# A three-part transformer block on one core: the opening rewritten, the sigmoid table loaded earlier, evictions moved ahead of weight splits

## The chip, the cores and the metric

The kernel runs on one NeuronCore of a Trainium2 chip. The metric is the device time of one execution in microseconds (us). TensorE does the matmuls, VectorE (DVE in the profile), ScalarE (ACT) and GpSimd (POOL) the rest, and SyncE (SP) issues most of the DMAs.

## The reference

Input x is 256 tokens by 1024 features, all fp32. The part that matters here is the first block's start, a recurrent branch, and beside it keys and values from a memory `mem_2` of 256 tokens:

```python
h = h + recurrent_block(rmsnorm(h, a_norm), a_w_in, a_conv_w, a_conv_b, a_w_gate, a_b_gate, a_lambda, a_w_out)

def recurrent_block(x, w_in, conv_w, conv_b, w_gate, b_gate, lam, w_out):
    u = x @ w_in
    gate, rec = u[..., :D_RNN], u[..., D_RNN:]
    rec = causal_depthwise_conv(rec, conv_w, conv_b)
    h = rg_lru(rec, w_gate, b_gate, lam)      # two sigmoids of rec @ w_gate, exp, sqrt, a scan over the tokens
    return (jax.nn.gelu(gate) * h) @ w_out
```

Behind it come an MLP of width 4096, a block of banded attention with another such MLP, and a third block with three kinds of attention, three gated branches, and a gated convolutional FFN of width 2816. None of that is touched by the change.

## The kernel before

**Numbers.** Every product is done in three passes. A weight w is split into a high part (a copy in the type fp32r, made by ScalarE) and a low part (w minus the high part, made by VectorE). The activations are split in the same way into the two halves of the tiles XA and XB. The product is then high times high, low times high and high times low.

**Weights.** They come in 163 units of 1 MB (128 x 2048), one after another, through four slots of `raw`, `whi` and `wlo`. SP issues the load of unit u once VectorE has finished the low part of unit u-4 (semaphore `s_lo`). ScalarE's `split(u)` (L617 to L638) waits for the landing, and for TensorE to be done with the slot; VectorE's `split(u)` (L1669 to L1690) waits for ScalarE's. Every engine's program is written out by hand in a fixed order. A split is done LEAD = 3 units ahead: while TensorE works on unit u, the splits of unit u+3 stand between the evictions of u. In the order of units, 0 to 3 are the recurrent half of `a_w_in` (U_REC), 4 the first quarter of its gate half, 5 the LRU gate weights (U_LRU), 6 to 8 the rest of the gate half, 9 and 10 the memory's keys (U_MEMK, called MEMK below), 11 and 12 its values (U_MEMV), 13 to 16 `a_w_out`.

**The opening.** SP loads x (L458), then unit 0 in two halves (L467), then seven of the small vectors (`BY_SP`), then units 1 to 3, then the memory rows (L488). ScalarE issues eleven small loads (L708), does four squares with a sum (L662) of x for the first norm, splits unit 0 in two halves (L716), copies the transposed vectors out of PSUM (L718) and makes the high parts of XA (L725). POOL makes the reciprocal roots (`roots`, L514 to L520), VectorE scales x (`norm`, L1698). TensorE runs matmuls of the identity with itself (`keep_warm`, L1195) until the data is there, transposes the two token halves of x (L1205), and between them, after waiting for all 18 small loads, the vectors (L1208 to L1211). VectorE makes the low parts of unit 0 (L1760) and of XA (L1765), then all of unit 1 (L1690). TensorE runs unit 0 with the contraction as its outer loop (L1222), then a small matmul for a table of biases (L1229), then units 1 to 4.

**The gates.** The products of U_REC are evicted by ScalarE (`rec_unit`, L736), convolved by VectorE (`conv`, L1789) and split into XB by `conv_hi` (ScalarE, L747) and `conv_lo` (VectorE, L1803). Then come eight gate products n = 0 to 7 (L1235 to L1246); product n waits for its low part (`s_cl`), and from n = 4 on for the two sigmoids of n-4 (L1239), because they share PSUM banks. The sigmoids are L784. `gate_out` (L752) evicts the groups of units 4 and 6 to 8, groups 8 to 15. The groups of MEMK, 16 to 19, need groups 12 to 15 out of their banks (L1083). `squares(SQ_NORM[1])` squares the memory rows on ScalarE (L662), `norm_hi` (L695) makes the high parts of XB for them, `decay` (L757) is exp and tanh, and L797 is the square root that `scan` (L1834) on VectorE waits for.

The lines before in ScalarE's order around the gates:

```python
split(U_GATE[0] + LEAD)
conv_hi(3)
act.wait_ge(s_ew, 32)
gate_out(0)
for n in range(8):
    ...
split(U_LRU + LEAD)
```

Of the kernel before, what the change touches and what calls it, by code (L numbers as in the profile page):

```python
# [13 lines left out]
P = 128  # L14
# [85 lines left out]
ROOTS = [2 * i for i in range(9)]  # L100
SUMS = [4 * i for i in range(7)] + [None, 28]
# [36 lines left out]
def bass_blocks(nc, A, out):  # L138
# [57 lines left out]
    with ctx:  # L196
# [112 lines left out]
        s_hi0, s_lo0, s_gain = sem("first_unit_half_hi"), sem("first_unit_half_lo"), sem("norm_gains")  # L309
        s_mem = sem("mem_loaded")  # L310
# [59 lines left out]
        BY_SP, BY_ACT = 7, 11  # L370
        WARM_UP, WARM_KEEP = 18, 4
# [53 lines left out]
        small_loads = []  # L425

        def small(dst, src):
            small_loads.append(lambda queue: queue.dma_start(dst, src).then_inc(s_small, 16))

        def vec(name, row, n):  # L430
            src = A[name].rearrange("a n -> (a n)") if len(A[name].shape) == 2 else A[name]
            small(rows_in[row:row + n, 0, :], src.rearrange("(k n) -> k n", n=P))

        vec("a_norm", R_ANORM, 8)
        vec("kv_norm", R_KV, 8)
        vec("b_norm", R_B, 8)
        vec("mlp_norm", R_MLP, 16)
        vec("norm_mix_pre_2", R_MIX, 8)
        vec("norm_ffn_pre_2", R_FFN, 8)
        vec("norm_mem_2", R_MEM, 8)  # L440
        vec("a_conv_b", R_CB, 8)
        small(rows_in[R_CW:R_CW + 32, 0, :], A["a_conv_w"][0].rearrange("w (k n) -> (w k) n", n=P))
        vec("a_lambda", R_LAM, 8)
        small(rows_in[R_BG:R_BG + 16, 0, :], A["a_b_gate"][0].rearrange("b (k n) -> (b k) n", n=P))
        fw = A["ffn_conv_w_2"][0].rearrange("w (k n) -> (w k) n", n=P)
        small(rows_in[0:88, 1, :], fw[0:88])
        small(rows_in[0:44, 2, :], fw[88:132])
        small(rows_in[44:88, 2, :], A["ffn_conv_b_2"][0].rearrange("(k n) -> k n", n=P))
        for r, name in enumerate(("k_norm", "b_q_norm")):
            src = A[name] if r == 0 else A[name][0]  # L450
            for half_ in range(2):
                small(rows_in[r:r + 1, 3, 64 * half_:64 * half_ + 64], src.rearrange("(a n) -> a n", a=1))
# [3 lines left out]
        def _(sp):  # L456
# [41 lines left out]
        def _(pool):  # L498
# [23 lines left out]
            def roots_deferred(b, col, power):  # L522

                pool.wait_ge(s_ss, 4 * b + 4)
# [11 lines left out]
            roots(SQ_NORM[0])  # L536
# [72 lines left out]
        def _(act):  # L609
# [43 lines left out]
            def squares(b, src, ready):  # L653

                for i, (t, c, bank) in enumerate(pieces()):
# [64 lines left out]
            act.wait_ge(s_xnT, XT_OF[0] + 1)  # L720
            for k in range(KT):
# [45 lines left out]
            rec_unit(1)  # L767
            conv_hi(0)
# [1496 lines left out]
```

## Time and profile before

| what | value |
|---|---|
| runs before | 1027.12, 1028.32, 1030.39 us; median 1028.32 |
| the profiled execution's own time | 1027.62 us |
| its span, from the first to the last instruction | 1025.7 us |
| TensorE's mean granted clock | 0.995 of full speed |
| busy share of TensorE, VectorE, ScalarE, POOL | 97%, 68%, 53%, 8% |
| share of the chain that ended last | PE 87%, DVE 7%, ACT 3%, issue 2%, DMA 1% |

"Busy" of TensorE counts a matmul from its start to a modelled end, so matmuls that follow each other without a gap show as 100%. In the timeline, "x2" merges neighbouring instructions of a kind; the bracket at the end of a row is the idle time just before it and what ended that by the profile. L-numbers are lines of the kernel.

### The profile page before, as it was taken

To read this page: it belongs to the slowest core of one execution; us is meant where nothing else is said; L and a number is where in the kernel's file an instruction comes from. 1 tells how busy PE (TensorE), PEld (TensorE's weight loads), DVE (VectorE), ACT (ScalarE), POOL (GpSimd) and SP (SyncE) were. 2 spreads that over 40 slices of the span, in tenths; PEclk is the share of its full clock that TensorE was granted. 3 is DMA by queue.
4 is the path that set the end of the run, shared out by engine and by line. 5 is a ranking of instruction groups with operands and counts; after the bars stand their busy time and mean duration, and the time that the engine had idled before them with its cause. 6 is when DMAs were issued, how large, how long until landed. Compare 5 with 4: busy or idle time off the path is not lost.

```text
span 1025.7 us, 15612 instructions
## 1 busy us (share of the span) xinstructions
PE 999.3 (97%) x6234; PEld 885.6 (86%) x6234; DVE 699.6 (68%) x1023; ACT 548.6 (53%) x804; POOL 83.8 (8%) x104
## 2 busy tenths in 40 slices
PE   8999999999999989999999999999999989999997
PEld 7998888888887866888888899989999879999996
DVE  5969566565667588575656565488665759877775
ACT  6897454444446477454444453356554456545452
POOL 2710010000002210020000000000004210000000
PEclk9999999999999999999999999999999999999999
DMA  9736586555535614565555647453454625655531
GB/s 319 227 122 206 166 316 214 172 196 200 170 122 176 235 50 165 183 219 173 196 201 169 203 124 234 135 165 125 124 165 152 226 75 188 223 174 197 179 110 41
DMA packets 120306, 180.39 MB, mean 176 GB/s; under 512 B 3145, under 2 KB 93609, under 8 KB 120249
## 3 DMA queue, kind: packets, MB, share of 16 engines
q1 hardware_dynamic: 118384, 174.11, 51.2%
q0 software_dynamic: 1536, 5.36, 1.5%
q8 instruction: 40, 0.66, 0.3%
q10 hardware_dynamic: 329, 0.12, 0.1%
q14 instruction: 17, 0.14, 0.0%
HBM read 178.48 MB, written 1.10 MB: 175 GB/s over the span
## 4 chain that ended last, share of the span: by engine, by line
PE 87%; DVE 7%; ACT 3%; issue 2%; DMA 1%; SPq 0%; POOL 0%; DVEq 0%; POOLq 0%; ACTq 0%
PE PS L1090 29%; PE PS L1154 28%; PE PS L1097 11%; PE PS L1099 5%; DVE wlo L1690 3%; PE PS L1347 2%; PE PS L1304 2%; PE PS L1444 2%; PE PS L1143 1%; PE PS L1594 1%; DVE arena L1795 1%; PE PS L1426 1%; PE PS L1395 1%; PE PS L1124 1%; DMA arena<-in_norm_mem 1%
## 5 line engine op out<-in xcount | busy, mean ns | idle before, releaser
L1690 DVE TENSOR_TENSOR wlo<-raw,whi 128x2048 fp32r<-128x2048 f32 x154 | 354.3, 2305 | 122.7 <-ACT whi L638 122.1
L638 ACT ACTIVATE whi<-raw 128x2048 fp32r<-128x2048 f32 x153 | 291.9, 1910 | 140.2 <-PE PS L1154 100.4
L1090 PE MATMUL PS<-XA,whi 128*128 128x256 f32 x1520 | 278.0, 285 | 0.3 <-DVE wlo L1690 0.3
L1090 PEld LDWEIGHTS PS<-XA,whi 128*128 128x128 f32 x1520 | 237.6, 192 | 3.9 <-issue 1.7
L1090 PE MATMUL PS<-XA,wlo 128*128 128x256 f32 x760 | 214.9, 283 | 0.0
L1154 PE MATMUL PS<-whi,XB 128*128 128x512 f32 x736 | 209.4, 391 | 0.7 <-DVE XB L1887 0.7
L1097 PE MATMUL PS<-XA,whi 128*128 128x512 f32 x512 | 182.1, 398 | 0.0
L1154 PEld LDWEIGHTS PS<-whi,XB 128*128 128x128 f32 x736 | 135.3, 188 | 29.3 <-issue 1.0
L1090 PEld LDWEIGHTS PS<-XA,wlo 128*128 128x128 f32 x760 | 145.6, 192 | 0.0
L1099 PE MATMUL PS<-XA,wlo 128*128 128x256 f32 x512 | 143.7, 281 | 0.0
L1154 PE MATMUL PS<-wlo,XB 128*128 128x512 f32 x368 | 117.6, 390 | 0.0
L1097 PEld LDWEIGHTS PS<-XA,whi 128*128 128x128 f32 x512 | 96.2, 188 | 23.6 <-issue 0.4
L1099 PEld LDWEIGHTS PS<-XA,wlo 128*128 128x128 f32 x512 | 96.7, 189 | 1.1
L1154 PEld LDWEIGHTS PS<-wlo,XB 128*128 128x128 f32 x368 | 69.1, 188 | 14.6
L827 ACT ACTIVATE arena<-PS 128x256 f32<-128x256 f32 x64 | 24.2, 381 | 89.1 <-PE PS L1099 89.0
L1876 DVE TENSOR_TENSOR arena<-PS,arena 128x256 f32<-128x256 f32 x64 | 26.4, 420 | 38.4 <-ACT arena L827 38.4
L1090 PE MATMUL PS<-XB,whi 128*128 128x256 f32 x256 | 46.4, 284 | 1.6 <-issue 1.6
L1304 PE MATMUL PS<-whi,XA 128*128 128x512 f32 x128 | 43.9, 408 | 1.0 <-DVE wlo L1690 1.0
L1055 ACT ACTIVATE arena<-arena,fvec 128x256 f32<-128x256 f32 x44 | 25.6, 596 | 35.2 <-DVE arena L2214 35.2
L1090 PEld LDWEIGHTS PS<-XB,whi 128*128 128x128 f32 x256 | 39.9, 192 | 2.0 <-issue 2.0
L2200 DVE SCALAR_TENSOR_TENSOR arena<-arena,fvec 128x256 f32<-128x256 f32 x88 | 38.6, 481 | 1.4 <-ACT arena L1055 0.7
L526 POOL TENSOR_SCALAR ss<-ss 128x1 f32<-128x1 f32 x8 | 2.5, 308 | 438.3 <-ACT arena L692 437.9
(240 smaller groups left out, 1223.3 us busy)
## 6 DMA issues: line engine op xcount, KB each, us to landing
raw<-in_w_up SPq DMA_DIRECT2D x32, 1024.0 KB, 5.5
raw<-in_w_down SPq DMA_DIRECT2D x32, 1024.0 KB, 4.9
raw<-in_w_ffn_up SPq DMA_DIRECT2D x22, 1024.0 KB, 5.0
raw<-in_w_in SPq DMA_DIRECT2D x21, 1024.0 KB, 5.1
raw<-in_w_ffn_down SPq DMA_DIRECT2D x11, 1024.0 KB, 4.8
raw<-in_w_kv SPq DMA_DIRECT2D x8, 1024.0 KB, 5.0
raw<-in_a_w_in SPq DMA_DIRECT2D x7, 1024.0 KB, 7.8
raw<-in_w_mem_kv SPq DMA_DIRECT2D x4, 1024.0 KB, 5.0
```

What stands on the lines that cost most here:

```text
L638: act.activation(whi[:, s, :], raw[:, s, :], ACT.Copy).then_inc(s_hi, 1)
L827: act.activation(dst, PS[:, bank_of(g), T:2 * T], ACT.Copy).then_inc(s_low, 1)
L1055: act.activation(fc[:, f, :], fu[:, f, 2:2 + T], ACT.Identity, scale=fvec[:, 1, c:c + 1], bias=fvec[:, 1, 44 + c:45 + c]).then_inc(s_fc, 1)
L1090: ins = pe.matmul(PS[:, bank_of(g), 0:T], w[:, k, P * m:P * m + P], X[:, k0 + k, part, :], start=(i == 0 and part == 0 and w is hi), stop= ...
L1097: pe.matmul(PS[:, bank, :].rearrange("p (e n) -> p e n", e=2), hi, x, start=opens, stop=False, skip_group_check=True)
L1099: return pe.matmul(PS[:, bank, 0:T], lo, x[:, 0, :], start=False, stop=closes, skip_group_check=True)
L1154: return pe.matmul(PS[:, bank + n * t + c, 0:width], X[:, k0 + k, part, P * t:P * t + P], w[:, k, c0 + 512 * c:c0 + 512 * c + width], star ...
L1304: ins = pe.matmul(PS[:, t_banks[t], :], X[:, 4 * i + k, part_, P * t:P * t + P], w[:, k, :], start=(i == 0 and k == 0 and part_ == 0 and w ...
L1347: ins = pe.matmul(PS[:, Q_BANKS[t][c], :], XB[:, 2 * i + k, part_, P * t:P * t + P], w[:, k, 512 * c:512 * c + 512], start=(i == 0 and k = ...
L1690: dve.tensor_tensor(wlo[:, s, :], raw[:, s, :], whi[:, s, :].bitcast(F32), ALU.subtract).then_inc(s_lo, 1)
L1876: dve.tensor_tensor(dst, PS[:, bank_of(g), 0:T], dst, ALU.add).then_inc(s_evac, 1)
L2200: ins = dve.scalar_tensor_tensor(fc[:, f, :], fu[:, f, i:i + T], fvec[:, 0, c:c + 1], fc[:, f, :], ALU.mult, ALU.add)
```

## The change

The first norm's squares go half to ScalarE (columns 0 to 511) and half to VectorE (512 to 1023, a multiply with a running sum), with semaphores of their own, and POOL waits for both. `a_norm` is loaded first, by ScalarE, and transposed and copied on its own ahead of x's transposes; the other vectors are transposed between unit 0 and unit 1 and copied after split(2). A dummy square ahead of ScalarE's other small loads brings the first table in; SP has ten small loads, ScalarE seven besides a_norm. The load of the memory rows goes from behind unit 3 to behind unit 5. Units 0 and 1 are both split in halves, the halves woven into XA's high parts, and TensorE runs both with the contraction outermost. The matmuls of `keep_warm` are 15, 3 and 3 instead of 18 and 4. A dummy sigmoid after `rec_unit(1)` brings the sigmoid table in. `conv_hi(3)` goes from ahead of the sigmoids to behind those of n = 1, `gate_out(0)` behind them all; `gate_out(2)` and `gate_out(3)` go ahead of the splits they stood behind. On VectorE `conv_lo(3)` goes ahead of `split(U_GATE[0] + LEAD)`.

```diff
-        BY_SP, BY_ACT = 7, 11
-        WARM_UP, WARM_KEEP = 18, 4
+        N_SMALL = 17
+        WARM_UP, WARM_BETWEEN, WARM_KEEP = 15, 3, 3
@@ SP
                 if u == 0:
-                    for load_small in small_loads[:BY_SP]:
-                        load_small(sp)
-                if u == 3:
+                    for dst, src in SMALL_BY_SP:
+                        sp.dma_start(dst, src).then_inc(s_small, 16)
+                if u == 5:

                     sp.wait_ge(s_xnT, 1)
@@ POOL
-            roots(SQ_NORM[0])
+            for t in range(TT):
+                pool.wait_ge(s_sq0, t + 1)
+                pool.wait_ge(s_sq1, t + 1)
+                link(pool.tensor_scalar(ss[:, 4 + t:5 + t], ss[:, 2 * t:2 * t + 1], ss[:, 2 * t + 1:2 * t + 2], EPS, ALU.add,
+                                        ALU.add))
+                pool.tensor_tensor(rstd[:, t:t + 1], ss[:, 4 + t:5 + t], mhalf[:, 0:1], ALU.pow).then_inc(s_root0, 1)
@@ ScalarE
-            for load_small in small_loads[BY_SP:]:
-                load_small(act)
-
-
-            squares(SQ_NORM[0], res, lambda i: act.wait_ge(s_x[i // 2], 16))
-            for h, done in enumerate((s_hi0, s_hi)):
-                act.wait_ge(s_landed[0] if h else s_w0, 16)
+            dst, src = vec("a_norm", R_ANORM, 8)
+            act.dma_start(dst, src).then_inc(s_an, 16)
+            act.wait_ge(s_zero, 1)
+            act.activation(snmax[:, 0, 0:1], smax[:, 0, 0:1], ACT.Square)
+            for dst, src in SMALL_BY_ACT:
+                act.dma_start(dst, src).then_inc(s_small, 16)
+
+            def first_half(w, h, done):
+
                 at = slice(UNIT // 2 * h, UNIT // 2 * h + UNIT // 2)
-                act.activation(whi[:, 0, at], raw[:, 0, at], ACT.Copy).then_inc(done, 1)
-            act.wait_ge(s_vT, 1)
-            act.activation(vecs[:], PS[:, 6, 0:P], ACT.Copy).then_inc(s_gain, 1)
+                act.activation(whi[:, w, at], raw[:, w, at], ACT.Copy).then_inc(done, 1)
+
+            for t in range(TT):
+                act.wait_ge(s_x[t], 16)
+                act.activation(av[:, 4 * t:4 * t + 2, :].rearrange("p a b -> p (a b)"), res[:, t, 0:512], ACT.Square,
+                               scale=D ** -0.5, accum_out=ss[:, 2 * t:2 * t + 1]).then_inc(s_sq0, 1)
+            act.wait_ge(s_w0, 16)
+            first_half(0, 0, s_hi0)
+            act.wait_ge(s_anT, 1)
+            act.activation(vecs[:, R_ANORM:R_ANORM + 8], PS[:, 6, 448:456], ACT.Copy).then_inc(s_gain, 1)
...
-                if k == 4:
-                    split(1, part=0)
-            split(1, part=1)
+                if k == 3:
+                    act.wait_ge(s_landed[0], 16)
+                    first_half(0, 1, s_hi)
+                if k == 5:
+                    act.wait_ge(s_landed[1], 16)
+                    first_half(1, 0, s_hi0)
+            first_half(1, 1, s_hi)
             split(2)
+            act.wait_ge(s_vT, 1)
+            act.activation(vecs[:, 8:P], PS[:, 6, 8:P], ACT.Copy).then_inc(s_vecs, 1)
+            act.wait_ge(s_vecs, 1)
...
             rec_unit(1)
+            act.activation(snmax[:, 0, 0:1], smax[:, 0, 0:1], ACT.Sigmoid)
             conv_hi(0)
...
             split(U_GATE[0] + LEAD)
-            conv_hi(3)
-
             act.wait_ge(s_ew, 32)
-            gate_out(0)
             for n in range(8):

+                if n == 2:
+                    conv_hi(3)
...
                 ins.then_inc(s_lru, 1)
+            gate_out(0)
...
+            gate_out(2)
             split(U_GATE[2] + LEAD)
-            gate_out(2)
...
+            gate_out(3)
             split(U_GATE[3] + LEAD)
-            gate_out(3)
@@ TensorE
             keep_warm(WARM_UP)
+            pe.wait_ge(s_an, 16)
+            pe.transpose(PS[:, 6, 448:456], rows_in[0:8, 0, :], ident[0:8, 0:8]).then_inc(s_anT, 1)
             for t in range(TT):
...
                 if t == 0:
-                    pe.wait_ge(s_small, 16 * (BY_SP + BY_ACT))
+                    keep_warm(WARM_BETWEEN)
+            ins.then_inc(s_xnT, 1)
+            keep_warm(WARM_KEEP)
+            for u in range(2):
...
+                if u == 0:
+
+                    pe.wait_ge(s_small, 16 * N_SMALL)
+                    pe.wait_ge(s_gain, 1)
                     pe.transpose(PS[:, 6, 0:P], rows_in[:, 0, :], ident[:])
...
+                    pe.wait_ge(s_tables, 16 * 4)
+                    pe.matmul(PS[0:16, 7, 0:384], relb[0:32, :], onehot[0:32, :], start=True, stop=True).then_inc(s_eps, 1)
+
+            for i in range(2, 4):
                 unit_a(U_REC[i], G_REC[i])
@@ VectorE
+            dve.memset(smax[:, 0, 0:1], 0.0).then_inc(s_zero, 1)
...
+                dve.tensor_tensor_reduce(junk, v, v, 1.0 / D, 0.0, ALU.mult, ALU.add, ss[:, 2 * t + 1:2 * t + 2])\
+                   .then_inc(s_sq1, 1)
...
-            split(1)
+            first_lo(1, 0, s_hi0, s_lo0)
+            first_lo(1, 1, s_hi, s_lo)
+            dve.wait_ge(s_vecs, 1)
             dve.tensor_copy(fvec[:, :, :], PS[:, 6, P:P + 176].rearrange("p (a b) -> p a b", a=2))
...
+            conv_lo(3)
             split(U_GATE[0] + LEAD)
-            conv_lo(3)
```

## Rows read from the trace of the kernel before

**Rows 1.** The page, part 1: busy time and share of the span, by engine.

```profile
PE 999.3 (97%) x6234; PEld 885.6 (86%) x6234; DVE 699.6 (68%) x1023; ACT 548.6 (53%) x804; POOL 83.8 (8%) x104
```

**Rows 2.** Timeline of TensorE: start and length in us, engine, line, operation.

```profile
11.59 1.97 PE L1205 MATMUL PS<-ident,arena 128*128 128x128 f32 x8
...
21.94 0.51 PE L1090 MATMUL PS<-XA,whi 128*128 128x256 f32 x2 [0.26 <-DVE wlo L1690]
...
45.08 0.28 PE L1243 MATMUL PS<-XB,whi 128*128 128x256 f32 x1
...
50.12 0.35 PE L1243 MATMUL PS<-XB,whi 128*128 128x256 f32 x1 [2.01 <-DVE XB L1806]
...
73.90 0.48 PE L1090 MATMUL PS<-XB,whi 128*128 128x256 f32 x2 [1.61 <-issue]
```

**Rows 3.** Busy time in two stretches: length, engines, granted clock, DMA share, GB/s.

```profile
12.20:12.80 0.60, 0.60 (x5) 0.60 (x4) 0.25 (x1) 0.00 (x0) 0.60 (x2) 0.50 1.11 362
26.00:35.00 9.00, 9.00 (x78) 9.00 (x77) 8.86 (x14) 7.43 (x13) 8.09 (x11) 1.00 0.89 281
```

**Rows 4.** The chain that ended last, two of its pieces before 120 us.

```profile
5.08 5.87 DMA arena<-in_norm_mem
...
85.64 31.48 PE PS L1154 x138
```

**Rows 5.** Timeline of ScalarE from 44 us on.

```profile
44.14 1.90 ACT L638 ACTIVATE whi<-raw 128x2048 fp32r<-128x2048 f32 x1
46.47 0.81 ACT L750 ACTIVATE XB<-arena 128x256 fp32r<-128x256 f32 x2 [0.42 <-DVE arena L1795]
47.19 0.64 ACT L643 ACTIVATE arena<-PS 128x256 f32<-128x256 f32 x2
47.85 1.28 ACT L784 ACT_TABLE_LOAD   x1
49.14 5.94 ACT L784 ACTIVATE arena<-PS,vecs 128x256 f32<-128x256 f32 x16
...
71.62 1.90 ACT L638 ACTIVATE whi<-raw 128x2048 fp32r<-128x2048 f32 x1
...
130.48 0.62 ACT L692 ACTIVATE arena<-res 128x512 f32<-128x512 f32 x1
```

**Rows 6.** Timeline of ScalarE in the opening.

```profile
5.15 1.28 ACT L662 ACT_TABLE_LOAD   x1 [5.15 <-issue]
6.44 0.63 ACT L662 ACTIVATE arena<-res 128x512 f32<-128x512 f32 x1
...
8.91 1.99 ACT L716 ACTIVATE whi<-raw 128x1024 fp32r<-128x1024 f32 x2
...
13.66 0.84 ACT L725 ACTIVATE XA<-PS,vecs 128x256 fp32r<-128x256 f32 x2 [1.69 <-PE PS L1205]
```

**Rows 7.** Timeline of POOL and of VectorE in the opening.

```profile
9.96 0.57 POOL L520 TENSOR_TENSOR rstd<-ss,mhalf 128x1 f32<-128x1 f32 x1
10.56 0.75 DVE L1698 TENSOR_SCALAR arena<-res,rstd 128x1024 f32<-128x1024 f32 x1 [0.85 <-POOL rstd L520]
...
21.80 0.33 DVE L1768 COPY fvec<-PS 128x176 f32<-128x176 f32 x1
```

**Rows 8.** DMA issues of small windows: size of one, us from issue to landing.

```profile
res<-in_x SPq DMA_DIRECT2D x1, 512.0 KB, 3.7
...
res<-in_x SPq DMA_DIRECT2D x1, 512.0 KB, 4.7
...
raw<-in_a_w_in SPq DMA_DIRECT2D x1, 1024.0 KB, 13.1
...
arena<-in_mem SPq DMA_DIRECT2D x1, 1024.0 KB, 8.7
```

**Rows 9.** Groups by line and shape: VectorE's multiply-reduce, busy us, mean ns.

```profile
L1972 DVE CUSTOM_DVE_ANT_0 arena<-PS,arena 128x256 f32<-128x256 f32 x32 | 13.4, 420 | 0.0
```

**Rows 10.** Timeline of VectorE from 76 us on.

```profile
76.48 1.23 DVE L1838 TENSOR_TENSOR arena<-arena 128x1024 f32<-128x1024 f32 x1 [0.63 <-ACT arena L797]
...
88.42 2.28 DVE L1690 TENSOR_TENSOR wlo<-raw,whi 128x2048 fp32r<-128x2048 f32 x1
```

More of the change, by code:

```diff
@@ L99 @@
 SQ_POST = [6, 8]
-ROOTS = [2 * i for i in range(9)]
-SUMS = [4 * i for i in range(7)] + [None, 28]
+ROOTS = [None] + [2 * i for i in range(8)]
+SUMS = [None] + [4 * i for i in range(6)] + [None, 24]
 KO = [0, 4, 1, 5, 2, 6, 3, 7]
@@ L423, in bass_blocks, with row_of @@
         NORM_HI = [8 * n + (8 if n > 3 else 0) for n in range(8)]
-        small_loads = []
-        def small(dst, src):
-            small_loads.append(lambda queue: queue.dma_start(dst, src).then_inc(s_small, 16))
+        def row_of(A_):
+            return A_.rearrange("a n -> (a n)") if len(A_.shape) == 2 else A_
         def vec(name, row, n):
-            src = A[name].rearrange("a n -> (a n)") if len(A[name].shape) == 2 else A[name]
-            small(rows_in[row:row + n, 0, :], src.rearrange("(k n) -> k n", n=P))
@@ L434, in bass_blocks @@
[L434 to L444, printed above, removed]
@@ L445, in bass_blocks @@
-        fw = A["ffn_conv_w_2"][0].rearrange("w (k n) -> (w k) n", n=P)
[L446 to L452, printed above, removed]
+            return rows_in[row:row + n, 0, :], row_of(A[name]).rearrange("(k n) -> k n", n=P)
@@ L455, in _ @@
+        SMALL_BY_SP = (vec("kv_norm", R_KV, 8), vec("b_norm", R_B, 8), vec("mlp_norm", R_MLP, 16),
+                       vec("norm_mix_pre_2", R_MIX, 8), vec("norm_ffn_pre_2", R_FFN, 8), vec("norm_mem_2", R_MEM, 8))
+        for r, src in enumerate((A["k_norm"], A["b_q_norm"][0])):
+            SMALL_BY_SP += tuple((rows_in[r:r + 1, 3, 64 * e:64 * e + 64], src.rearrange("(a n) -> a n", a=1)) for e in range(2))
         @block.sync
@@ L522, in roots_deferred @@
             def roots_deferred(b, col, power):
-                pool.wait_ge(s_ss, 4 * b + 4)
+                pool.wait_ge(s_ss, SUMS[b] + 4)
                 for t in range(TT):
@@ L1206, in _ @@
                 if t == 0:
-                    pe.wait_ge(s_small, 16 * (BY_SP + BY_ACT))
+                    keep_warm(WARM_BETWEEN)
+            ins.then_inc(s_xnT, 1)
+            keep_warm(WARM_KEEP)
+            for u in range(2):
+                g = G_REC[u]
+                hi, lo = W8(whi, u % SLOTS), W8(wlo, u % SLOTS)
+                for k in range(KT):
+                    if k % 4 == 0:
+                        pe.wait_ge(*((s_lo0, u + 1) if k == 0 else (s_lo, u + 1)))
+                    if u == 0:
+                        pe.wait_ge(s_xlo, NORM_HI[0] + k + 1)
+                    for m in range(2):
+                        for w, part in ((hi, 0), (hi, 1), (lo, 0)):
+                            ins = pe.matmul(PS[:, bank_of(g + m), 0:T], w[:, k, P * m:P * m + P], XA[:, k, part, :],
+                                            start=(k == 0 and part == 0 and w is hi), stop=(k == KT - 1 and w is lo),
+                                            skip_group_check=True)
+                        if k == KT - 1:
+                            ins.then_inc(s_step, 1)
+                if u == 0:
+                    pe.wait_ge(s_small, 16 * N_SMALL)
+                    pe.wait_ge(s_gain, 1)
                     pe.transpose(PS[:, 6, 0:P], rows_in[:, 0, :], ident[:])
@@ L1211, in _ @@
                     pe.transpose(PS[:, 6, 384:386], rows_in[0:2, 3, :], ident[0:2, 0:2]).then_inc(s_vT, 1)
-            ins.then_inc(s_xnT, 1)
-            keep_warm(WARM_KEEP)
-            u, g = U_REC[0], G_REC[0]
-            hi, lo = W8(whi, u % SLOTS), W8(wlo, u % SLOTS)
-            for k in range(KT):
-                if k % 4 == 0:
-                    pe.wait_ge(*((s_lo0, 1) if k == 0 else (s_lo, u + 1)))
-                pe.wait_ge(s_xlo, NORM_HI[0] + k + 1)
-                for m in range(2):
-                    for w, part in ((hi, 0), (hi, 1), (lo, 0)):
-                        ins = pe.matmul(PS[:, bank_of(g + m), 0:T], w[:, k, P * m:P * m + P], XA[:, k, part, :],
-                                        start=(k == 0 and part == 0 and w is hi), stop=(k == KT - 1 and w is lo),
-                                        skip_group_check=True)
-                    if k == KT - 1:
-                        ins.then_inc(s_step, 1)
-            pe.wait_ge(s_tables, 16 * 4)
-            pe.matmul(PS[0:16, 7, 0:384], relb[0:32, :], onehot[0:32, :], start=True, stop=True).then_inc(s_eps, 1)
-            for i in range(1, 4):
+                    pe.wait_ge(s_tables, 16 * 4)
+                    pe.matmul(PS[0:16, 7, 0:384], relb[0:32, :], onehot[0:32, :], start=True, stop=True).then_inc(s_eps, 1)
+            for i in range(2, 4):
                 unit_a(U_REC[i], G_REC[i])
```

29 lines of the change are left out of this document (24 added, 5 removed).

## The prediction

> **What bounds the kernel now.** I read the page first: TensorE is busy for 97% of the span [rows 1]. So nothing counts unless it moves TensorE's work forward in time, and after the opening a microsecond gained or lost stays to the end. Next TensorE's own timeline, for its gaps [rows 2]: between the first matmul and 75 us it waits three times: 0.26 at 21.94 ahead of unit 1 (for the weight's low part), 2.0 at 50.12 after the fourth of the eight gate products, which began at 45.08, and 1.6 at 73.90 ahead of the first MEMK product. Then the windows [rows 3]: from 26 to 35 us VectorE is busy 8.86 of 9.00 us. VectorE sets the pace there, not ScalarE (7.43). Its order is split, convolution, low parts, four times over, all without a gap; whatever it gains at the opening arrives whole at the gate products. The chain [rows 4] adds that the opening starts with a wait for the last small load, landing at 10.95, and that from 85.64 TensorE runs 138 wide matmuls in a row, 0.228 us each.
>
> The wait at 50.12 needs care. The trace names VectorE's L1806, but the product that waits is n=4, and that needs the sigmoids of n=0 (L1239). They begin at 49.14, because of an eviction of 0.64 and a table load of 1.28 ahead of them [rows 5]; a pair takes 5.94/8 = 0.74, so they end at 49.9. Both causes end together; to gain here, both must go, and the change moves both. The wait at 73.90 is for the eviction of group 12, which stands at 73.42 behind a split that starts at 71.62 [rows 5].
>
> **The opening, part by part.** Before [rows 6]: table load 5.15, four squares from 6.44 at 0.63 each, the last accumulator read near 9.0; POOL's second root ends at 10.53, VectorE's second xn runs 10.56 to 11.31 [rows 7], and the second transposes end at 13.56, with a granted clock of 0.50 (1.2 GHz) [rows 2, 3]. ScalarE's first XA high part is at 13.66 [rows 6].
>
> After: ScalarE issues one load (0.6), then does the table load and a dummy square (1.5), then seven loads (before they and four others filled 0.73 to 5.12, about 0.40 each, so 2.9). If these are serial, its first square starts at 5.8; if the loads are issued while the table loads, at 4.5, when x lands (0.73 + 3.7) [rows 8]. The second half of x lands 5.9 (1.17 + 4.7). VectorE does the other two squares: 128x512 isn't in the trace; L1972 takes 0.42 for 256 elements [rows 9], so between 0.42 and 0.84 plus its read of 0.08. I take 0.7, hidden beside ScalarE in the serial case. ("Lead" below is how much earlier than before the same work comes.) Serial: both ScalarE squares end at 7.2; POOL's two roots, 0.95 and 1.42 as before, end at 9.1; xn of the second half ends at 9.9, 1.4 earlier. Without the four small transposes (0.5) in between, the second transposes start at 10.0. They take 1.1 at the full clock and 1.97 at the lower level. So the first XA high part is at 11.15 or 12.0, a lead of 2.5 or 1.65.
>
> From there to fvec (21.80 before, 8.14 after the first high part [rows 6, 7]) the same work runs, in other order: unit 0's second half (1.0, from 1.99 for two [rows 6]) now stands between ScalarE's high parts 3 and 4, and VectorE waits 0.55 for it; unit 1 in halves recovers the 0.47 that VectorE waited for its whole split; and VectorE waits 0.4 more for the vector copy, now behind split(2). Net 0.6 lost. **VectorE's lead after the opening: 1.9 (full clock) or 1.05 (lower), serial.** With the loads under the table load, the roots start 1.3 earlier but the second half of x lands only at 5.9, so xn is 0.9 earlier: 2.75 or 1.9. I take 1.9, the value that two of the four combinations give.
>
> TensorE: unit 0 starts at 12.3 but waits for VectorE's parts, ends near 18.7; four transposes (0.66) and L1229 (0.8) now stand between unit 0 and 1, so unit 1 starts at 20.2 instead of 21.94, lead 1.75. Unit 1 with its high and low halves is fed in time.
>
> The moved DMAs: SP issues ten small loads instead of seven ahead of unit 1, 1.2 us later at most, one of them (a_norm) gone to ScalarE. Unit 3 was issued from 6.25 and landed 13.1 later [rows 8], units 1 to 3 landing 3 us apart at 13.3, 16.3, 19.3: the stream is full, so the delay costs between 0 and 1.2, covered by 1.5 us until ScalarE takes each. The mem load moves behind units 4 and 5 and their waits; it took 8.7 to land [rows 8], would land near 29, and its first reader comes at 39.8. Units 4 and 5 land 3 us earlier. Nothing.
>
> **The gate products.** Leads 1.9 (VectorE) and 1.75 (TensorE): the products start at 43.35, n=3 ends at 46.2. ScalarE's split(7), at 44.14 before [rows 5], now ends at 44.1; sigmoids 0 and 1 follow at 44.2 (the sigmoid table is loaded after rec_unit(1), where ScalarE waited 1.26 for VectorE). Then conv_hi(3), whose source VectorE finished at 46.8 - 1.9 = 44.9, then sigmoids 2 to 7. n=4 finds the sigmoids of n=0 at 45.0; conv_lo(3) without unit 7's split (2.2) ahead of it ends at 46.9, and n=6 wants it at 47.6. So the 2.0 wait is gone, the eight end at 49.1 against 53.1, and TensorE's lead is 4.0.
>
> ScalarE: 44.2 + 5.7 (sigmoids) + 0.72 (conv_hi) + 0.64 (gate_out(0)) = 51.3 at the next split, which stood at 54.85: **ScalarE's lead 3.6** (1.9, plus the table load 1.28, plus 0.43 that it waited at 46.47). gate_out(0) is free where it is now: group 12 needs it at 56. Everything on ScalarE up to 71.62 moves with it. There gate_out(2) comes first: group 12 is out at 68.0 + 0.5 = 68.5, TensorE arrives at 72.3 - 4.0 = 68.3. MEMK starts 5.4 earlier. gate_out(3), due for TensorE at 74.2, is out at 74.1.
>
> **What is late next.** VectorE's chain from the square root: 76.48 multiply, then scans, unit 11, y, and unit 12's split ending at 90.7, with no gap [rows 10]. It hangs on ScalarE's square root, which keeps its place behind norm_hi, one split and one eviction: lead 3.6. TensorE wants unit 12 24 x 0.228 = 5.5 after 85.54, at 91.05: slack 0.35. With a lead of 5.4 it arrives at 85.6 and unit 12 is ready at 87.1. It waits 1.5, and keeps 3.6 + 0.35 = **4.0 us**, to the end: behind it TensorE is the bound and the others wait for it.
>
> **Sum.** 1027.62 (profiled run; span 1025.70 and 1.92 around it) - 4.0 = 1023.6. The median of the runs shown is 0.7 above that run, so I give 1028.3 - 4.0 = **1024.3**. The four combinations of the opening give 3.1, 4.0, 4.0 and 4.9.
>
> On the table: between ScalarE's instruction before it and its first sigmoid lie 1.28 us and no more (47.85 to 49.14 [rows 5]). The Trainium skill, "ScalarE: Activation LUTs", What ACT_TABLE_LOAD costs, puts a drain of 1.38 on top of 1.28; by that the hoisted load would be worth 2.66 and the sum 1.4 more. The trace doesn't show that drain.
>
> **Rivals.**
> *The opening's lead is lost.* TensorE now waits for a_norm ahead of all transposes. It is issued first, but if it lands as late as the last small load did (10.95 [rows 4]), the first high part comes at 14, VectorE's lead is -0.8 and the gain 1.3: 1027.0. Against it: it stands ahead of every other load on its queue. Chance 0.12.
> *Square reloads a table.* Squares of the mem rows now run after the sigmoid table is in. If that set lacks Square, two loads of 1.28 come back: gain 4.0 - 2.55 = 1.45, 1026.9. Against it: Squares run at 130.48 without a load, long after a Gelu table came in [rows 5]. Chance 0.06. The Trainium skill's same page, Table sets, names copy, identity, relu and abs as present in every set and tells to batch by set; Square isn't among those it names.
> *TensorE keeps all.* If unit 12 is ready anyway, because VectorE's tail has slack that I read as work, the gain is 5.3: 1023.0. Against it: that stretch shows no idle time. Chance 0.05.
> *Slower.* The start-up has 21 filler matmul calls instead of 22 and other gaps. The clock fell to 0.50 at 11.6 and was back at 15.2, under the first matmuls. If it stays at the lower level through unit 0, that unit's 48 matmuls take 5.76 more (0.12 to 0.24): unit 1 starts at 26.0, the gain is used up (n=4 at 52.05 against 50.12, less the wait of 1.6): nothing gained. If it stays through unit 1 too, another 5.76: 1034. This decides only from 5.8 us of delay on. Against it: matmuls without a gap brought it back in 3 us before. Chance 0.05.
> *The forecast.* 0.72, its own range 1023.4 to 1025.2.
>
> **How the numbers follow.** A measurement of this kernel can tell about 0.3% (3.1 us) from no change: faster is below 1025.2. Of the forecast's 0.72, 0.60 lie there (its slow-clock serial end and run-to-run spread fall short). Faster 0.60 + 0.05 = 0.65; same 0.12 + 0.12 + 0.06 = 0.30; slower 0.05. The range goes from 1023.0 less the runs' spread of 0.7, 1022.3, to the first rival's 1027.0.
>
> **What would show it.** First square near 4.5 or 5.8; first XA high part at 11 to 12; fvec copy at 19 to 20.8; no table load between split(7) and the first sigmoid, and no wait over 0.3 in the gate products; MEMK's first matmul at 68.5; a new TensorE wait of 1 to 2 us near 85.6 ahead of unit 12, released by L1690's counterpart. If that wait is missing the gain is over 5; if a table load stands ahead of the mem squares, or a_norm lands after 8, it is under 2. Behind 95 us the two traces should run parallel; a gain that shrinks there makes the forecast wrong.

## The result and the profile after

The changed kernel takes **1023.31 us** in the median of 5 runs (1022.90 to 1024.28), against 1028.34 for the kernel before in 5 runs (1027.12 to 1030.39): a ratio of 0.995, 95% interval 0.9937 to 0.9963. The profiled execution took 1023.31 with a span of 1021.1; the profiled one of before took 1027.62 with 1025.7. So the two profiles differ by 4.6 in the span, the medians by 5.0; when both were run again (below), the medians differed by 4.2. 1024.3 was predicted, with a range of 1022.3 to 1027.0.

On the page the busy times have hardly moved [rows 1]; the span lost idle time of TensorE:

```profile
PE 998.4 (98%) x6233; PEld 884.8 (87%) x6233; DVE 704.3 (69%) x1029; ACT 547.9 (54%) x803; POOL 85.1 (8%) x104
```

TensorE's timeline (start, length, engine, line, operation, idle time before it) answers to [rows 2]. There are the two groups of transposes, the first product of unit 0, the first of unit 1, the first gate product, the first MEMK product, the first MEMV product (unit 11) and the first of unit 13:

```profile
7.70 1.09 PE L1222 MATMUL PS<-ident,arena 128*128 128x128 f32 x8
...
9.30 1.09 PE L1222 MATMUL PS<-ident,arena 128*128 128x128 f32 x8
...
11.72 0.47 PE L1237 MATMUL PS<-XA,whi 128*128 128x256 f32 x2 [0.65 <-DVE XA L1807]
...
19.42 0.50 PE L1237 MATMUL PS<-XA,whi 128*128 128x256 f32 x2
...
42.55 0.28 PE L1266 MATMUL PS<-XB,whi 128*128 128x256 f32 x1
...
67.67 0.47 PE L1105 MATMUL PS<-XB,whi 128*128 128x256 f32 x2 [0.19 <-issue]
...
81.11 0.47 PE L1169 MATMUL PS<-whi,XB 128*128 128x512 f32 x1 [1.71 <-ACT kT_me L641]
...
92.10 0.61 PE L1169 MATMUL PS<-whi,XA 128*128 128x512 f32 x2
```

The waits of 2.0 and 1.6 are gone. A new one of 1.71 stands ahead of MEMV, not of unit 12. The second group of transposes takes 1.09, not 1.97: the granted clock is 1.00 from 9.30 to 10.39, where it was 0.50 for the same work [rows 3].

ScalarE's timeline answers to [rows 5, 6]. The small loads (rows of ACTq) are issued while the table loads; the sigmoid table comes in at 26.70, and the squares of the memory rows at 38.97 and the sigmoids at 43.53 have no table load ahead of them:

```profile
1.38 1.28 ACT L709 ACT_TABLE_LOAD   x1 [1.38 <-PEq L2298]
1.45 0.28 ACTq L711 DMA_DIRECT2D arena<-in_a_conv_b  x1
...
4.94 0.63 ACT L720 ACTIVATE arena<-res 128x512 f32<-128x512 f32 x1 [2.07 <-DMA res<-in_x]
...
10.50 0.84 ACT L732 ACTIVATE XA<-PS,vecs 128x256 fp32r<-128x256 f32 x2 [1.45 <-PE PS L1222]
...
26.70 1.28 ACT L782 ACT_TABLE_LOAD   x1
27.99 0.20 ACT L782 ACTIVATE snmax<-smax 128x1 f32<-128x1 f32 x1
...
38.97 0.62 ACT L660 ACTIVATE arena<-arena 128x512 f32<-128x512 f32 x1
...
41.42 1.90 ACT L636 ACTIVATE whi<-raw 128x2048 fp32r<-128x2048 f32 x1
43.53 1.58 ACT L798 ACTIVATE arena<-PS,vecs 128x256 f32<-128x256 f32 x4 [0.20 <-PE PS L1268]
...
50.40 2.05 ACT L636 ACTIVATE whi<-raw 128x2048 fp32r<-128x2048 f32 x1
...
76.62 2.01 ACT L818 ACTIVATE arena<-arena 128x1024 f32<-128x1024 f32 x2
78.53 1.90 ACT L636 ACTIVATE whi<-raw 128x2048 fp32r<-128x2048 f32 x1
80.33 0.64 ACT L641 ACTIVATE kT_me<-PS 128x256 f32<-128x256 f32 x2
```

VectorE's timeline answers to [rows 7, 10]: the first of its two squares, the fvec copy, the multiply behind the square root, and unit 12's split. The last two come 4.43 earlier than before.

```profile
4.50 0.69 DVE L1786 CUSTOM_DVE_ANT_0 arena<-res 128x512 f32<-128x512 f32 x1 [3.58 <-DMA res<-in_x]
...
19.08 0.34 DVE L1812 COPY fvec<-PS 128x176 f32<-128x176 f32 x1 [0.32 <-ACT vecs L743]
...
72.05 1.23 DVE L1882 TENSOR_TENSOR arena<-arena 128x1024 f32<-128x1024 f32 x1
...
83.99 2.28 DVE L1713 TENSOR_TENSOR wlo<-raw,whi 128x2048 fp32r<-128x2048 f32 x1
```

**Where the time came from.** VectorE's lead at fvec is 21.80 - 19.08 = 2.72. ScalarE's next split after the sigmoids stood at 54.85 and now stands at 50.40: lead 4.45, that is 2.72 plus 1.73 gained at the gates. The table load gives 1.29 of that and conv_hi(3)'s wait 0.42; 0.22 comes from instructions standing closer together, and 0.2 is lost in the new wait at 43.53. TensorE's lead at unit 13 is 96.54 - 92.10 = 4.44. The spans differ by 4.6, so nothing is given back behind it.

**The edge.** Four rows of the kernel before show why TensorE keeps 4.44. First its ScalarE, then its TensorE, at the point of the new wait:

```profile
73.42 0.65 ACT L643 ACTIVATE arena<-PS 128x256 f32<-128x256 f32 x2
...
84.76 0.64 ACT L643 ACTIVATE kT_me<-PS 128x256 f32<-128x256 f32 x2
```

```profile
85.54 0.47 PE L1154 MATMUL PS<-whi,XB 128*128 128x512 f32 x1
96.54 0.62 PE L1154 MATMUL PS<-whi,XA 128*128 128x512 f32 x2
```

The first MEMV product waits for MEMK's keys to be evicted into kT_me. It started 0.78 behind that eviction's start (85.54 - 84.76); in the changed kernel also 0.78 (81.11 - 80.33). Before, TensorE came at the same instant, so the timeline showed no idle time. Both go back to one eviction, that of group 12 at 73.42: TensorE starts MEMK 0.48 behind it and MEMV 11.64 after that, and ScalarE reaches kT_me 11.34 after it; 0.48 + 11.64 - 11.34 is 0.78. So the eviction of kT_me stood on the edge all along, and TensorE can be no earlier than it.

### The profile page after: what moved, and what is told of

Its sections match the earlier page's. It is cut to its first block, busy times and chain, and to the rows that moved or that the text cites. A ratio compares the mean times of both kernels' runs of the same rounds, so it can differ in the third digit from the quotient of the medians.

```text
span 1021.1 us, 15617 instructions
## 1 busy us (share of the span) xinstructions
PE 998.4 (98%) x6233; PEld 884.8 (87%) x6233; DVE 704.3 (69%) x1029; ACT 547.9 (54%) x803; POOL 85.1 (8%) x104
## 3 DMA queue, kind: packets, MB, share of 16 engines
q0 software_dynamic: 1536, 5.36, 1.6%
## 4 chain that ended last, share of the span: by engine, by line
PE 88%; ACT 6%; DVE 4%; issue 2%; POOL 0%; DVEq 0%; POOLq 0%; ACTq 0%
PE PS L1169 28%; PE PS L1105 28%; PE PS L1112 11%; PE PS L1114 5%; PE PS L1370 2%; PE PS L1327 2%; PE PS L1467 2%; PE PS L1158 1%; DVE wlo L1713 1%; PE PS L1617 1%; PE PS L1449 1%; ACT whi L636 1%; PE PS L1237 1%; PE PS L1418 1%; PE PS L1139 1%
## 5 line engine op out<-in xcount | busy, mean ns | idle before, releaser
L1105 PE MATMUL PS<-XA,whi 128*128 128x256 f32 x1488 | 272.2, 285 | 0.0
L1105 PEld LDWEIGHTS PS<-XA,whi 128*128 128x128 f32 x1488 | 232.6, 192 | 3.0 <-issue 1.7
L1105 PE MATMUL PS<-XA,wlo 128*128 128x256 f32 x744 | 210.4, 283 | 0.0
L1114 PE MATMUL PS<-XA,wlo 128*128 128x256 f32 x512 | 143.7, 281 | 0.0
L1105 PEld LDWEIGHTS PS<-XA,wlo 128*128 128x128 f32 x744 | 142.5, 192 | 0.0
L1112 PEld LDWEIGHTS PS<-XA,whi 128*128 128x128 f32 x512 | 96.2, 188 | 23.8 <-issue 0.4
L1114 PEld LDWEIGHTS PS<-XA,wlo 128*128 128x128 f32 x512 | 96.7, 189 | 1.1
```

The lines of the kernel that those rows point to most:

```text
L1105: ins = pe.matmul(PS[:, bank_of(g), 0:T], w[:, k, P * m:P * m + P], X[:, k0 + k, part, :], start=(i == 0 and part == 0 and w is hi), stop= ...
L1112: pe.matmul(PS[:, bank, :].rearrange("p (e n) -> p e n", e=2), hi, x, start=opens, stop=False, skip_group_check=True)
L1114: return pe.matmul(PS[:, bank, 0:T], lo, x[:, 0, :], start=False, stop=closes, skip_group_check=True)
```

## The experiments

"Unit 13" below is the start of its first product, 96.54 before and 92.10 after. It is the sharpest ruler here: the end of a run also carries the spread of some 900 us behind it. The profiles show one source of it, the granted clock: all 14 profiles have a stretch at 0.50 between 824 and 836 us, and all but that of e8 one between 360 and 384, some 3 to 7 us long from profile to profile.

### One half of the change at a time

The gates alone, on the old opening, and the opening alone, with the old order at the gates and no early sigmoid. The gates alone (e1) are the kernel before with these lines (on ScalarE, and the last ones on VectorE) and a zeroed tile for the dummy sigmoid; the opening alone (e2) is the changed kernel with the same lines undone:

```diff
             rec_unit(1)
+            act.activation(snmax[:, 0, 0:1], smax[:, 0, 0:1], ACT.Sigmoid)
...
-            conv_hi(3)
-
             act.wait_ge(s_ew, 32)
-            gate_out(0)
             for n in range(8):
+                if n == 2:
+                    conv_hi(3)
...
+            gate_out(0)
...
+            gate_out(2)
             split(U_GATE[2] + LEAD)
-            gate_out(2)
...
+            gate_out(3)
             split(U_GATE[3] + LEAD)
-            gate_out(3)
...
+            conv_lo(3)
             split(U_GATE[0] + LEAD)
-            conv_lo(3)
```

> The kernel before, with the gates' part of the change alone: sigmoid table early, conv_hi(3) behind the sigmoids of n=1, gate_out(0) behind them all, gate_out(2) and gate_out(3) ahead of their splits, conv_lo(3) ahead of unit 7's split. Theory A (the two parts add up as leads of ScalarE): the table load's 1.28 us and the 0.43 that ScalarE waited for VectorE go, ScalarE reaches norm_hi 1.7 earlier, no wait of 2.0 at the fourth gate product, gain 1.7 to 2.0: about 1026.4. Rival B (the gates' part pays only behind an earlier opening, because VectorE's own chain from 15 to 50 us is untouched): under 0.5 us, 1027.9 or more.

> The changed kernel with the gates' part put back as it was before; only the new opening is left. Theory A: VectorE's lead of 2.7 us at the fvec copy arrives whole at the gates, the waits of 2.0 and 1.6 us stay, and the gain is 2.7: about 1025.6. Rival B (the opening carries the whole gain): 1024 or less. Rival C (TensorE's later waits swallow the opening): 1027.5 or more.

Measured, beside the kernel before at 1028.58 (24 runs): gates alone 1026.41 (ratio 0.998, 0.9971 to 0.9989), unit 13 at 93.69; opening alone 1026.56 (0.9979, 0.997 to 0.9987), unit 13 at 94.42. The gains, 2.2 and 2.0, add up to 4.2, as much as the changed kernel gained when it was run again (1028.12 - 1023.95, below), and less than the 5.0 of its first runs. In each the kT_me eviction is the edge: 81.91 and 82.63, and unit 13 stands 11.78 and 11.79 behind it. Of the gates' half, the moves of `conv_hi(3)`, `gate_out(0)` and `conv_lo(3)` were not tried one by one.

The opening alone keeps the wait at the gates, and behind it the clock falls. Its TensorE timeline, and its windows (length; busy time of PE, PEld, DVE, ACT, POOL; granted clock; DMA share; GB/s):

```profile
47.47 0.36 PE L1265 MATMUL PS<-XB,whi 128*128 128x256 f32 x1 [1.82 <-DVE XB L1849]
```

```profile
48.00:50.00 2.00, 2.00 (x12) 2.00 (x11) 1.04 (x2) 2.00 (x7) 0.41 (x1) 0.50 0.86 216
50.00:52.00 2.00, 2.00 (x13) 2.00 (x13) 0.00 (x0) 1.69 (x5) 1.97 (x1) 0.66 0.83 316
```

That fall has a price, and the expectation of 2.7 arriving whole missed it. ScalarE's splits ahead of the sigmoids and behind them stand at:

```profile
41.49 1.90 ACT L636 ACTIVATE whi<-raw 128x2048 fp32r<-128x2048 f32 x1
...
52.84 1.91 ACT L636 ACTIVATE whi<-raw 128x2048 fp32r<-128x2048 f32 x1
```

The first has the whole lead of the opening (44.14 - 41.49 = 2.65), the second 2.01 (54.85 - 52.84); unit 13 has 2.12. So 0.6 went between them, in the stretch of the slow clock. The times fit: the five runs of this kernel with a mean clock of 0.995 or more took 1024.36 to 1026.11, the seven at 0.993 or less 1026.44 to 1027.38. The mean takes in the falls behind 95 us too, so this alone does not place the loss.

And the gates alone ran with the old opening, but without the fall at 11.6 that the profile of before had [rows 3]. Its second transposes took 1.09, and fvec came at 20.89 instead of 21.80; in e7, again the old opening without the fall, at 21.15. So 0.65 to 0.9 of the 2.72 that the changed opening shows against the profile of before is a clock fall that this one execution had. Against e7's unit 13 (95.90, below) the changed kernel is 3.80 earlier, not 4.44. That is close to what separates the fastest runs: 1026.59 of all 59 of the kernel before, 1022.90 of the ten of the changed one.

### Waits against the clock behind them

If each wait is followed by a fall, part of the gain would be clock and not wait. The wait at the gates was filled with matmuls in the kernel before (e7), and the fillers were taken out of the opening of the changed one (e8):

The first diff is of the kernel before, the second of the changed one:

```diff
             for n in range(8):
...
+                if n == 4:
+                    pe.wait_ge(s_evac, G_REC[3] + 2)
+                    for _ in range(8):
+                        pe.matmul(PS[:, 2, 0:P], ident[:], ident[:], start=True, stop=True, skip_group_check=True)
```

```diff
-        WARM_UP, WARM_BETWEEN, WARM_KEEP = 15, 3, 3
+        WARM_UP, WARM_BETWEEN, WARM_KEEP = 15, 0, 0
```

> The kernel before, with eight filler matmuls of the identity put into TensorE's wait of 2.0 us at the fourth gate product; nothing else moves. Theory C (part of the change's gain is that TensorE no longer stands still there: in some executions the granted clock falls to 0.50 behind that wait, as the profile of e2_opening_only shows from 48 to 51 us): median 0.5 to 1.5 below the kernel before and its slowest runs gone (before: 1026.7 to 1030.3). Rival D: the spread has another source; median and spread as before, 1028.5.

> The changed kernel without the fillers between and behind the transposes of x (3 and 3 calls become 0 and 0). Theory C: TensorE stands still for 0.7 and 1.3 us in the opening, the granted clock falls to 0.50 there for about 3 us in some or all executions, unit 0 ends up to 1.5 later, and the time is 0.5 to 1.5 above the changed kernel, with a wider spread. Rival D: unit 0 is paced by VectorE's low parts, so nothing is lost: 1023.3.

Measured, beside the kernel before at 1027.51 (15 runs): filled, 1027.62 (1.0001, 0.9992 to 1.001). The wait was 0.23 and the clock 1.00 from 46 to 52; but in the profile of the kernel before it is 1.00 behind its wait of 2.01 too. So filling gains nothing measurable in this kernel; e2's wait, with the fall behind it, was not filled in any run. Unit 13 came 0.64 earlier, at 95.90, and so had fvec (21.15, 0.65 earlier): this opening too ran at full clock. Without fillers 1023.68 (0.9961, 0.9947 to 0.9974), unit 13 at 92.95: no fall either, though TensorE idled 1.32 ahead of unit 0. What made it 0.85 later was a DMA. Its ScalarE timeline:

```profile
18.16 1.91 ACT L636 ACTIVATE whi<-raw 128x2048 fp32r<-128x2048 f32 x1 [1.60 <-DMA raw<-in_a_w_in]
```

Unit 2's weights landed late, fvec went to 20.27, and kT_me to 81.17. Over the ten profiles of kernels with the new opening and its order of loads, split(2) did not wait for this landing in seven, and 0.46, 0.59 and 1.60 in three.

### The table load and the evictions

Two diffs of the changed kernel, one without the early sigmoid (e3), one with gate_out(2) and gate_out(3) behind their splits (e4):

```diff
             rec_unit(1)
-            act.activation(snmax[:, 0, 0:1], smax[:, 0, 0:1], ACT.Sigmoid)
```

```diff
-            gate_out(2)
             split(U_GATE[2] + LEAD)
+            gate_out(2)
...
-            gate_out(3)
             split(U_GATE[3] + LEAD)
+            gate_out(3)
```

> The changed kernel without the dummy sigmoid behind rec_unit(1), so that the table is loaded ahead of the first real sigmoid. Theory A: ScalarE's chain is the bound from the gates to the memory products, so the 1.28 us come back in full: 1024.6, and the load stands at about 43.5 with TensorE waiting 1.1 us after the fourth gate product. Rival: by the Trainium skill's page on ScalarE a switch costs 2.66 with its drain: 1026.0. Rival: hidden beside VectorE: no change from the changed kernel.

> The changed kernel with gate_out(2) and gate_out(3) behind their splits again. Theory A: TensorE waits some 1.8 us more at the first MEMK product (start 69.5), but the wait of 1.7 at 81.1 ahead of MEMV shrinks by the same, because the eviction into kT_me comes at the same time: no change (within 0.3 us of the changed kernel). Rival: the wait taken away at MEMK is a gain of its own: 1.6 to 1.8 slower, 1025.

Measured: without the early sigmoid 1025.09 (0.9968, 0.9956 to 0.9979), unit 13 at 93.58, 1.48 later; the load of 1.28 stood at 43.75, and TensorE waited 0.6 for sigmoids. Of the 1.48, 0.25 stood there before the load, at the split ahead of it (41.67 against 41.42), so the load itself is worth 1.23. With the two evictions behind their splits 1024.10 (0.9958, 0.9945 to 0.9971), unit 13 at 92.00. That is nothing lost, although TensorE now waits longer at MEMK:

```profile
69.36 0.47 PE L1105 MATMUL PS<-XB,whi 128*128 128x256 f32 x2 [2.16 <-issue]
```

kT_me is evicted at 80.22 all the same, and 81.00 - 80.22 is 0.78 again. The wait at MEMK and the wait at MEMV are one budget, and both end with ScalarE. "Gate evictions first", the part of the change that removes the 1.6 us wait at 73.90 [rows 2], gives nothing by itself. It is not idle in every order, though: with a start at 69.36 TensorE reaches MEMV at 81.00 and no earlier, so the order of e6 below, which starts MEMV at 79.16, needs this step. That is worked out from rows; no run puts the two together.

### The new wait: two things that are late together

First the keys' evictions went ahead of unit 12's split (e5); then VectorE's unit-12 split went ahead of y as well (e6; `split(U_MEMK + LEAD)` on ScalarE is unit 12's):

```diff
-            for h in range(2):
-                split(U_MEMK + h + LEAD)
+            def mem_out(h):
                 for m in range(2):
                     evac(G_MEMK + 2 * h + m, BEFORE(U_MEMK + h) + m + 1, kT_me[:, 2 * h + m, :])
+
+            mem_out(0)
+            split(U_MEMK + LEAD)
+            split(U_MEMK + 1 + LEAD)
+            mem_out(1)
```

On VectorE, in the second kernel alone, from behind y to ahead of it:

```diff
+            split(U_MEMK + LEAD)
...
-            split(U_MEMK + LEAD)
```

> The changed kernel with ScalarE's evictions of groups 16 and 17 (kT_me) ahead of unit 12's split instead of behind it. Theory A (the prediction's: unit 12's low part is late by the same amount, so the wait only moves): MEMV starts at 79.4 without the wait of 1.7 but TensorE then waits 1.3 ahead of unit 12 for L1713; gain 0.35 over the changed kernel, 1023.0. Rival B (only the eviction is late): gain 1.7, 1021.6.

> As e5_mem_eviction_first, and on VectorE unit 12's split ahead of the two products y_out instead of behind them. Theory A: both late things are out of the way, neither wait is left before 95 us, gain 1.7 over the changed kernel, 1021.6. Rival: y then comes late for unit 13 and the wait moves there, 1023.

Measured, beside the same runs of the kernel before as e7 and e8 (1027.51): 1023.75 (0.9958, 0.9944 to 0.9971) for the first, and the wait comes back one unit later, where the prediction had put it. The list of TensorE's waits up to 130 us (us in total, times, longest):

```profile
PE PS L1173 <- DVE wlo L1717: 1.3, 1, 1.3
```

MEMV starts at 79.07, 2.04 earlier, but unit 13 at 91.66 only 0.44 earlier, 0.20 of which is this profile's opening (unit 7's split on ScalarE at 41.22 against 41.42). No gain in time over the changed kernel is measurable. With both moved, the list has no wait over 0.2 between MEMK and 130 us, kT_me is evicted at 78.38 and unit 13 comes at 90.14:

```profile
78.38 0.64 ACT L641 ACTIVATE kT_me<-PS 128x256 f32<-128x256 f32 x2
```

The time is **1022.30** (1021.27 to 1022.96; 0.9945, 0.9931 to 0.9958), 1.4 below e5 and e8, which ran beside it, with unit 13 1.96 earlier than in the changed kernel. It beats the kernel before. The changed kernel did not run beside it, and the two ratios' intervals overlap (0.9931 to 0.9958 and 0.9937 to 0.9963); that it beats this one too rests on unit 13 and on e5 and e8.

### What in the opening matters

The changed kernel again (e9), the reordered one with SP's ten small loads behind unit 3 (e10), the changed one with all squares on ScalarE (e11), and the changed one with unit 1 split whole (on VectorE; TensorE then waits for the whole low part; e12). One diff for each of the last three (cut: in e11 POOL waits for two sums of `s_sq0` instead of one of each engine):

```diff
-                if u == 0:
+                if u == 3:
                     for dst, src in SMALL_BY_SP:
```

```diff
-                act.activation(av[:, 4 * t:4 * t + 2, :].rearrange("p a b -> p (a b)"), res[:, t, 0:512], ACT.Square,
-                               scale=D ** -0.5, accum_out=ss[:, 2 * t:2 * t + 1]).then_inc(s_sq0, 1)
+                for c in range(2):
+                    act.activation(av[:, 4 * t + 2 * c:4 * t + 2 * c + 2, :].rearrange("p a b -> p (a b)"),
+                                   res[:, t, 512 * c:512 * c + 512], ACT.Square,
+                                   scale=D ** -0.5, accum_out=ss[:, 2 * t + c:2 * t + c + 1]).then_inc(s_sq0, 1)
...
-            for t in range(TT):
-                first_squares(t)
```

```diff
-            first_lo(1, 0, s_hi0, s_lo0)
-            first_lo(1, 1, s_hi, s_lo)
+            split(1)
```

> The changed kernel itself once more, so that the three beside it have their reference on the same chip. Both theories: 1023.3 +- 0.5, unit 13's first product at 92.1, and 92.9 in a profile in which unit 2's weights land late in the opening. TensorE's wait of 1.7 at L1169 behind ScalarE's eviction of kT_me stands.

> The reordered kernel e6 with SP's ten small loads issued behind unit 3's weights, not behind unit 0's. Theory: the small loads hold up the weights that follow them, so units 1 to 3 land earlier, ScalarE's split of unit 2 (L636) waits for no landing, VectorE's wait ahead of the fvec copy falls to 0.3 or less; unit 13's first product at 90.1 or up to 0.5 earlier, 1022.0 +- 0.6. Rival: the small vectors now land too late for ScalarE's copy of vecs and VectorE's copy of fvec: a new wait of 1 to 3 there, unit 13 at 91 or later, and the time is back at 1023 to 1025.

> The changed kernel with all four squares on ScalarE. Theory: the root of each half needs 0.63 more (one more square behind the other), and what follows in the opening goes by the second root: everything up to unit 13 is 0.6 later, unit 13 at 92.7, time +0.6 (1023.9). Rival: the weights' landings set the opening and squares are hidden: unit 13 at 92.1, no change. A rival's other side: both halves' squares are serial and 1.25 late: unit 13 at 93.4.

> The changed kernel with unit 1 split whole on VectorE and awaited whole by TensorE. Theory: unit 1 in halves brings little, since TensorE is busy with unit 0 until 19.4: VectorE's work is one instruction fewer, its end within 0.2 of the changed kernel's, unit 13 within 0.2 of 92.1 and the time within 0.2. Rival: TensorE starts unit 1 0.6 to 1.0 later, for the low half now comes whole: unit 13 at 92.7 to 93.1, time +0.6 to +1.0.

Measured, beside the kernel before at 1028.12 (15 runs):

| kernel | us | ratio (95%) | fvec | kT_me | unit 13 |
|---|---|---|---|---|---|
| changed, again | 1023.95 | 0.9959 (0.9946 to 0.9973) | 19.27 | 80.49 | 92.25 |
| e6 + small loads later | 1026.98 | 0.9988 (0.9979 to 0.9997) | 21.55 | 82.44 | 94.23 |
| one engine squares | 1023.80 | 0.9957 (0.9944 to 0.9971) | 19.31 | 80.54 | 92.30 |
| unit 1 whole | 1023.87 | 0.9958 (0.9945 to 0.9972) | 19.40 | 80.55 | 92.31 |

**Small loads later** went as its rival said, and worse. Unit 2 was there in time (split(2) at 17.00 with no wait), but the vectors were not. Its TensorE and its windows:

```profile
20.57 0.33 PE L1250 MATMUL PS<-ident,arena 128*128 128x128 f32 x1 [2.07 <-DMA arena<-in_b_q_norm]
```

```profile
20.00:24.00 4.00, 3.43 (x16) 2.65 (x17) 2.39 (x7) 1.86 (x3) 0.00 (x0) 0.73 1.07 350
24.00:28.00 4.00, 4.00 (x30) 4.00 (x30) 3.93 (x8) 3.69 (x6) 2.69 (x1) 0.85 1.03 375
```

The wait of 2.07 was followed by a clock fall, and unit 13 is 4.09 later than in e6. The fvec copy is 2.27 later, so 1.8 more was lost behind it, where the clock was down.

**Unit 1 in halves** gives nothing measurable, as expected: unit 13 is 0.06 later with it whole.

**Squares on two engines** give nothing either, against my expectation of 0.6. With one engine the first half's sum was ready at 5.96 instead of 5.36, as expected, so POOL's root started at 6.52 and not at 5.93. But that root took 1.11 in the changed kernel run again (e9). POOL in e9, then in the one-engine kernel:

```profile
5.93 1.11 POOL L534 TENSOR_TENSOR rstd<-ss,mhalf 128x1 f32<-128x1 f32 x1
```

```profile
6.52 0.57 POOL L533 TENSOR_TENSOR rstd<-ss,mhalf 128x1 f32<-128x1 f32 x1
```

They end at 7.04 and 7.09, and the second roots at 8.63 and 8.68. VectorE's second square is the neighbour: it ran from 5.92. And where the root ended early, TensorE's fillers held the transposes back. In the kernel with unit 1 whole it ended at 6.48 and xn was written from 6.58, but TensorE's fillers ahead of the transposes lasted to 7.84, and the first product of unit 0 came at 11.96, against 11.90 in e9 and 11.94 with one engine.

## Why the prediction was right, and where it was not

**Total: right, 1024.3 against 1023.31.** The signs of both large terms, the gain's order, and that nothing is given back behind 95 us, were right. The predicted gain of 4.0 was worked out against one profile. In the two profiles it is 4.44 at unit 13, with a clock fall in the opening of before; against e7's opening without it, 3.80. So the 4.0 lies between, partly by luck: two of its terms were off in opposite directions, as told below.

**The opening: right in its cases, low in the pick.** The four combinations gave 1.05, 1.9, 1.9 and 2.75. The one measured is the last, loads issued under the table load and full clock: 2.72. The first square came at 4.94, the second half of x set the pace (6.28 instead of 5.9), VectorE's square took 0.69 (0.7 taken), the first high part stood at 10.50 (11.15 or 12.0 predicted), fvec at 19.08. Inside that case two errors nearly cancel: the first high part was 0.25 later than the 10.25 that it gives (11.15 less 0.9), and the new order behind it lost 0.44, not 0.6. The mis-sized term was this 1.9. That the choice was open in the clock alone was shown by e1 and e7: the old opening at full clock puts fvec at 20.89 and 21.15, so against an execution without the fall the lead is 1.6 to 2.1, not 2.72.

**The vector copy's wait** was 0.32 (0.4 predicted). **Unit 1** started at 19.42, not 20.2, a lead of 2.52 against 1.75: the same 0.8.

**Landings: too bold.** That a delay of 0 to 1.2 is covered by the 1.5 until ScalarE takes each unit holds in seven of the ten profiles, but unit 2 landed 0.46, 0.59 and 1.60 too late in the others. In e8 TensorE's 0.85 of delay came from this term, which I had put at nothing.

**The gates: right.** The 2.0 wait is gone. ScalarE gained 1.73 there (1.71 predicted). The table load alone is worth 1.23 (e3). No drain: 26.70 + 1.28 = 27.98, and the next ACTIVATE starts at 27.99. The Trainium skill, "ScalarE: Activation LUTs", What ACT_TABLE_LOAD costs, adds about 1.38 for a drain, 2.66 in all. Neither this row nor e3's loss shows it.

**Evictions first: the end was right, the worth wasn't stated.** MEMK started at 67.67 (68.5 predicted) with no wait over 0.2. But e4 shows that this step moves no time.

**What is late next: the step that failed in its cause.** I put a wait of 1.5 ahead of unit 12, released by its low part, and let TensorE keep 3.6 + 0.35. It waited 1.71 ahead of unit 11's MEMV, for kT_me. I had not asked when MEMK's own evictions were due, since no row showed TensorE waiting for them. The slack there was 0, so TensorE keeps ScalarE's lead and no more: 84.76 - 80.33 = 4.43 against 4.44 at unit 13. The predicted wait does exist behind it: e5 shows 1.3. The amount, 4.0, came near by luck: the slack of 0.35 that was credited and isn't there, and the 0.8 by which the opening was put too low, have opposite signs.

**The rivals.** a_norm wasn't late (its transpose stood at 7.49, right behind the fillers). Squares ran at 38.97 without a load, under the sigmoid table. "TensorE keeps all" is excluded by the wait at MEMV. The clock did not fall in the changed opening's profiles, but it fell behind waits elsewhere (e2, e10).

**What stays open.** Why the clock falls behind one wait and not behind another wasn't settled. The old opening gives one hint: in the profile of before TensorE stood idle for 2.48 ahead of the first transposes, in e1 and e7, where no fall follows, for 1.38 and 1.28. The later load of the memory rows was not undone in any run; its first reader, at 38.97, did not wait. POOL's stretched root is put beside VectorE's square by time alone: e11 takes the square away, but moves the root's start too. The spread of unit 2's landing has no shown cause: moving the small loads took its wait away in one profile, as it was absent in seven others.

## What to carry to other kernels

Before you credit a removed wait, look at every semaphore that the slowest engine passes between there and the next bound, also those at which it does not idle: "no idle time" can mean a slack of zero. Find the instruction that sets the end (here one eviction on ScalarE: in 13 of 14 profiles unit 13 came 11.76 to 11.79 behind it, the other being e5 with its wait between them) and price each edit by how far it moves that one instruction. Sharing squares between engines and removing a wait that is taken again later moved nothing; taking a table load out of its way did (e3), and so did taking a split out of its way together with the next late one (e6).

## What the runs showed of the hardware

- **DMA issues run under a table load.** ScalarE's queue issued loads at 1.45, 1.76, 2.12 and 2.54 while its table load ran from 1.38 to 2.66.
- **The clock falls in some executions only.** The same second transposes took 1.97 at 0.50 in the profile of before, and 1.09 in e1 and e7. A stall of 1.82 (e2) and one of 2.07 (e10) were followed by a granted clock of 0.50 (48 to 50 us and 22 to 24); behind the wait of 2.01 in the kernel before and the one of 1.71 in the changed one the next two microseconds show 1.00.
- **POOL's power operation beside VectorE.** 128x1 takes 0.57, but 1.11, 1.12 and 0.99 in the three profiles in which it started at or behind the start of VectorE's square; in the other eight profiles of the new opening, in which it started earlier or no such square ran, 0.57.
